# A fused encoder step on Trainium2: the opening rebuilt around x and c handed over transposed

## The reference

```python
def rmsnorm(x, gain):
    xf = x.astype(jnp.float32)
    y = xf * lax.rsqrt(jnp.mean(xf * xf, axis=-1, keepdims=True) + EPS)
    return (y * gain.astype(jnp.float32)).astype(x.dtype)

def mixer_layer(x, c, pos, past, w_ada, b_ada, ln_gain, w_in, ...):
    mod = jnp.einsum('bd,de->be', jax.nn.silu(c), w_ada) + b_ada
    shift, scale, gate = jnp.split(mod, 3, axis=-1)
    h = rmsnorm(x, ln_gain) * (1 + scale[:, None]) + shift[:, None]
    proj = jnp.einsum('btd,de->bte', h, w_in)
    ...
    q_a, ckv, krope, g_a, q_b, k_b, v_b, q_i, k_i, w_i, g_b = jnp.split(proj, split_at, axis=-1)
    # group A: latent attention from q_a, ckv, krope; group B: top-k sparse attention from q_b, k_b, v_b, q_i, k_i, w_i
    y = jnp.concatenate([rmsnorm(o_a, out_gain_a) * jax.nn.silu(g_a),
                         rmsnorm(o_b, out_gain_b) * jax.nn.silu(g_b)], axis=-1)
    out = jnp.einsum('bte,ed->btd', y, w_out)
    return x + gate[:, None] * out, new_rows
```

## Time and profile before

| | |
|---|---|
| median of 3 runs | 923.52 us |
| profiled execution | 923.6 us, span 921.8 us |
| TensorE (PE) busy | 884.2 us, 96% |
| weight loads (PEld) | 763.3 us, 83% |
| VectorE (DVE) busy | 416.6 us, 45% |
| ScalarE (ACT) busy | 321.6 us, 35% |
| GpSimd (POOL) busy | 124.2 us, 13% |
| chain that ended last | PE 84%, DVE 2%, ACT 2% of the span |
| loads of `ada` units | 64 x 512 KB, all in the first eighth |

### The profile page before, as it was taken

How to read it: one execution, slowest core, us unless ns; L and a number is a source line. 1 busy time by engine, 2 the same in 40 slices (tenths; PEclk the granted TensorE clock), 3 DMA queues, 4 the chain that set the end, 5 groups by cost and what they waited for, 6 DMA issues and landing times.

```text
span 921.8 us, 13576 instructions
## 1 busy us (share of the span) xinstructions
PE 884.2 (96%) x5485; PEld 763.3 (83%) x5485; DVE 416.6 (45%) x847; ACT 321.6 (35%) x598; POOL 124.2 (13%) x192
## 2 busy tenths in 40 slices
PE   4799999999999999999999999999999999999996
PEld 1376788999998688888999888888988898778885
DVE  3522343336322145433331576238645466697362
ACT  3222343434322234322321344233233345544251
POOL 1000003101200000112220300003012124450000
PEclk9899999999999999999999999999999999999998
DMA  8999957474443222556543666547878743793413
GB/s 342 409 409 409 408 190 231 157 243 159 143 137 103 69 92 69 186 174 213 186 137 107 206 235 230 207 149 226 292 250 256 253 143 109 274 295 116 137 57 126
DMA packets 53599, 187.43 MB, mean 203 GB/s; under 512 B 7872, under 2 KB 8568, under 8 KB 52384
## 3 DMA queue, kind: packets, MB, share of 16 engines
q1 hardware_dynamic: 39632, 141.85, 43.6%
q0 software_dynamic: 13904, 44.71, 15.4%
HBM read 175.93 MB, written 12.69 MB: 205 GB/s over the span
## 4 chain that ended last, share of the span: by engine, by line
PE 84%; DVE 2%; ACT 2%; issue 1%; POOLq 0%; DVEq 0%; POOL 0%; ACTq 0%
PE proj L1755 33%; PE proj L1744 29%; PE proj L1771 2%; PE bankO L1850 1%; PE bankO L1859 1%; PE proj L1728 1%; PE bankS L1771 1%; PE bankS L1744 1%; DVE w_lo L1272 1%; PE bankS L1913 1%; PE bankO L1940 1%; PE bankO L1932 1%; PE bankO L1931 1%; PE bankO L1900 1%; PE bankS L1956 1%
## 5 line engine op out<-in xcount | busy, mean ns | idle before, releaser
L1272 DVE TENSOR_TENSOR w_lo<-raw,w_hi 128x1024 fp32r<-128x1024 f32 (+2 forms) x164 | 198.7, 1217 | 236.2 <-ACT w_hi L954 235.4
L954 ACT ACTIVATE w_hi<-raw 128x1024 fp32r<-128x1024 f32 (+2 forms) x164 | 167.4, 1027 | 188.8 <-PE proj L1744 109.6
L1755 PE MATMUL proj<-hT_hi,w_hi 128*128 128x384 f32 x608 | 210.8, 347 | 0.0
L1755 PE MATMUL proj<-hT_hi,w_lo 128*128 128x384 f32 x608 | 203.7, 335 | 0.0
L1755 PE MATMUL proj<-hT_lo,w_hi 128*128 128x384 f32 x608 | 203.4, 335 | 0.0
L1744 PE MATMUL proj<-w_hi,hT_hi 128*128 128x512 f32 (+2 forms) x464 | 178.5, 385 | 2.8 <-DVE w_lo L1272 1.5
L1744 PE MATMUL proj<-w_hi,hT_lo 128*128 128x512 f32 (+2 forms) x464 | 173.8, 375 | 0.0
L1744 PE MATMUL proj<-w_lo,hT_hi 128*128 128x512 f32 (+2 forms) x464 | 173.8, 374 | 0.0
L1755 PEld LDWEIGHTS proj<-hT_hi,w_hi 128*128 128x128 f32 x608 | 114.2, 188 | 9.4 <-issue 7.8
L1755 PEld LDWEIGHTS proj<-hT_lo,w_hi 128*128 128x128 f32 x608 | 114.3, 188 | 0.6 <-issue 0.2
L1755 PEld LDWEIGHTS proj<-hT_hi,w_lo 128*128 128x128 f32 x608 | 114.1, 188 | 0.0
(11 more groups left out here) (357 smaller groups left out, 1022.4 us busy)
## 6 DMA issues: line engine op xcount, KB each, us to landing
raw<-in_units SPq DMA_DIRECT2D x184, 512.0 KB, 3.7
araw<-in_units SPq DMA_DIRECT2D x64, 512.0 KB, 9.5
kcT<-in_dsa_k_t POOLq DMA_DIRECT2D x8, 512.0 KB, 5.8
vc<-in_cache_dsa_v POOLq DMA_DIRECT2D x8, 512.0 KB, 5.6
gate_scratch<-stage POOLq DMA_DIRECT2D x8, 384.0 KB, 3.3
raw<-in_units SPq DMA_DIRECT2D x8, 336.0 KB, 4.0
raw<-in_units SPq DMA_DIRECT2D x8, 320.0 KB, 5.0
x_sb<-in_x_prompt SPq DMA_DIRECT2D x2, 1024.0 KB, 6.6
```

Source lines behind the costliest of these rows:

```text
L954: return nc.scalar.activation(out, in_, func, scale=scale, **kw)
L1272: V.tensor_tensor(w_lo[:, SLOT[u], 0:w], raw_of(u)[:, 0:w], high(u)[:, 0:w].bitcast(F32), ALU.subtract).then_inc(lo_ready, 1)
L1755: ins = mm(banks[blk][:, 0:TOK], w[:, n, cols], a[:, kt, :], start=first and n == m == 0, stop=final and n == per - 1 and m == 2)
```

## The change

x and c are laid out transposed before the launch (`x_t`, `c_t`), and so are the gains and biases (`gains_t`). x is loaded straight into `xsT` in four parts of four blocks. The squares are taken there, two parts on ScalarE and two on VectorE, and summed over the partitions by 16 products with a matrix of ones into 32-row groups (`xss`); a second product with ones adds the groups (`rb`), ScalarE takes the root, VectorE the reciprocal, over 384 columns on all partitions. Eight multiplications (`xm`) then scale `xsT`, one per pair of blocks. The transposes of x and c are gone.

The first `ada` chunk becomes two, `ade` 0 and 1: eight units each, with two blocks by 256 shift and 256 scale columns in a unit, so products have 128 columns and there are eight per unit. Each gives one pair of blocks. The chunks `ga` 0 and 1 become one chunk `gp` of 512 columns: a unit covers two blocks and four banks, so it needs one pair. Product units now stand inside `ade` 1 and `ada` 1 to 3.

```diff
-    out = [("ada", q, 1, 1) for q in range(4)]
-    out += [("kb", 0, 2, NT), ("ga", 0, 4, 2), ("ga", 1, 4, 2), ("ckv", 0, 2, NT), ...]
+    out = [("ade", e, 2, 1) for e in range(2)] + [("ada", q, 1, 1) for q in range(1, 4)]
+    out += [("kb", 0, 2, NT), ("gp", 0, 2, 4), ("ckv", 0, 2, NT), ...]
...
-    out = of("ada", 0)
-    for q in range(1, 4):
-        ada = of("ada", q)
-        out += ada[:4] + [keys[2 * q - 2]] + ada[4:8] + [first[q - 1]] + ada[8:12] + [keys[2 * q - 1]] + ada[12:]
-        out.append(second[q - 1])
-    out += [keys[6], keys[7], first[3], second[3]]
+    half = of("ade", 1)
+    out = of("ade", 0) + half[:3] + [keys[0]] + half[3:6] + [gates[0]] + half[6:]
+    ada = of("ada", 1)
+    out += ada[:5] + [keys[1]] + ada[5:10] + [gates[1]] + ada[10:]
+    for q in range(2, 4):
+        ada, n = of("ada", q), 2 * q - 2
+        out += ada[:4] + [keys[n]] + ada[4:8] + [gates[n]] + ada[8:12] + [keys[n + 1]] + ada[12:] + [gates[n + 1]]
+    out += [keys[6], keys[7], gates[6], gates[7]]
...
-        order.insert(max(first, at - AHEAD), u)
+        order.insert(max(first, at - (3 if u < second else 5 if u < third else 6)), u)
...
-    put(0, ("xsq", 0), ("xsq", 1), ("xsq", 2), ("xr", 0))
+    put(0, ("xsq", 0), ("xsq", 1), ("xsq", 2), ("xsq", 3), ("xss", 0))
     put(1, ("rb", 0))
-    run(1, "xT", 6, 2)
-    run(2, "xS", 6, 2)
+    put(2, ("xm", 0), ("xm", 1))
+    for m in range(2, 8):
+        put(m + 1, ("xm", m))
...
+    for n, mod in enumerate(MODS):
+        u = LAST_UNIT[mod]
+        pairs = [m for m in range(KT // 2) if MOD_OF_PAIR[m] == n]
+        put(u, ("modT", n))
+        if n == 0:
+            put(u, ("first_hi", 0))
+        put(u, *(("h", m) for m in pairs))
+        if n == 0:
+            put(u, ("first_lo", 0))
+        put(u, *(("hl", m) for m in pairs))
...
+        for n in range(4):
+            blocks = slice(4 * n, 4 * n + 4)
+            sp.dma_start(xsT[:, blocks, :], i["x_t"][:, blocks, :]).then_inc(sem(f"x_in{n}"), 16)
...   # VectorE
+        def xsq(n):
+            if n % 2:
+                part = xsT[:, 4 * n:4 * n + 4, :]
+                dve.wait_ge(sem(f"x_in{n}"), 16)
+                V.tensor_tensor(xsqr[:, 4 * n:4 * n + 4, :], part, part, ALU.mult).then_inc(sem(f"x_sq{n}"), 1)
+        def rb(n):
+            emptied(dve, "rb", n)
+            link(V.reciprocal(rbc[:], rbc[:]))
+        def xm(m):
+            part = xsT[:, 2 * m:2 * m + 2, :]
+            V.tensor_tensor(part, part, rbc[:].unsqueeze(1).broadcast_to([P, 2, TOK]),
+                            ALU.mult).then_inc(sem("x_scaled"), 1)
...   # TensorE
+            if (kind, j) in MODS[1:] and first:
+                emptied(pe, "modT", MODS.index((kind, j)) - 1)
+        def xss(n):
+            out = take("xss", n, "S")
+            for q in range(4):
+                pe.wait_ge(sem(f"x_sq{q}"), 1)
+                for g in range(4):
+                    ins = mm(out[32 * g:32 * (g + 1), 0:TOK], ones[:, 0:32], xsqr[:, 4 * q + g, :], start=q == 0,
+                             stop=q == 3)
+            ins.then_inc(full["S"], 1)
```

More of the change, by code:

```diff
@@ L117, in rings @@
     for u, (c, _) in enumerate(UNITS):
-        ada = CHUNKS[c][0] == "ada"
+        ada = CHUNKS[c][0] in ("ade", "ada")
         slot = RAW + counts[1] % ARAW if ada else counts[0] % RAW
@@ L127 @@
 SLOT, SLOT_BEFORE = rings()
-AHEAD = 6
 def loads():
     order = list(range(len(UNITS)))
-    first, last = (UNITS.index((CHUNK_OF["ada", q], k)) for q, k in ((1, 0), (3, KT - 1)))
-    for u in [u for u in order if CHUNKS[UNITS[u][0]][0] != "ada" and u < last + 3]:
+    first = UNITS.index((CHUNK_OF["ade", 1], 0))
+    second = UNITS.index((CHUNK_OF["ada", 1], 0))
+    third = UNITS.index((CHUNK_OF["ada", 2], 0))
+    last = UNITS.index((CHUNK_OF["ada", 3], KT - 1))
+    for u in [u for u in order if CHUNKS[UNITS[u][0]][0] not in ("ade", "ada") and u < last + 3]:
         at = order.index(u)
         order.remove(u)
-        order.insert(max(first, at - AHEAD), u)
+        order.insert(max(first, at - (3 if u < second else 5 if u < third else 6)), u)
     return order
 LOADS = loads()
-WHOLE = ("ada", "gate")
+WHOLE = ("ade", "ada", "gate")
 SPLIT_UNITS = [u for u, (c, _) in enumerate(UNITS) if CHUNKS[c][0] not in WHOLE]
@@ L163, in banks @@
     for kind, j, _, nb in CHUNKS:
-        if kind == "ada":
+        if kind in ("ade", "ada"):
             mine = [NPB]
@@ L399, in packed_units @@
         dst = out[u, :, 0:per * n].reshape(P, per, n)
-        if kind == "ada":
+        if kind == "ade":
+            for a in range(2):
+                dst[:, :, 256 * a:256 * (a + 1)] = w_ada[:, ks, a * D + 256 * j:a * D + 256 * (j + 1)]
+        elif kind == "ada":
             for a in range(2):
@@ L1315, in modT_ @@
[L1315 to L1316 removed]
+            k0, k1 = MOD_BLOCKS[n]
+            w = 32 * (k1 - k0)
+            part = modT[:, :, k0:k1, :]
+            dve.wait_ge(sem("small_in"), 48)
+            b_cols = gcol[:, 32:64].rearrange("p (a k) -> p a k", a=2)[:, :, k0:k1]
             for a in range(2):
[L1318 to L1319 removed]
+                ins = V.tensor_tensor(part[:, a], bank["O"][:, w * a:w * (a + 1)].rearrange("p (k j) -> p k j", j=32)[:, :, 0:9],
+                                      b_cols[:, a].unsqueeze(2).broadcast_to([P, k1 - k0, 9]), ALU.add)
@@ L1722, in products @@
                 clear(0)
-                for g in range(4):
+                for n, g in itertools.product(range(2), range(4)) if kind == "ade" else ():
+                    cols = raw_of(u).rearrange("p (a n) -> p a n", a=2)[:, n, P * g:P * (g + 1)]
+                    ins = mm(banks[0][32 * g:32 * (g + 1), 0:P], cs[:, 2 * k + n, :], cols, start=first and n == 0,
+                             stop=final and n == 1)
+                for g in range(4) if kind != "ade" else ():
                     if kind == "ada":
@@ L1748, in products @@
             else:
-                for blk in range(2):
+                for blk in range(nb):
                     cols = slice(P * blk, P * (blk + 1))
```

210 lines of the change are left out of this document (78 added, 132 removed), and 2 rows, old and new, of the table STEP_BANKS.

## The result

The changed kernel takes 928.58 us in the median of six runs (928.15 to 931.77); the kernel before takes 923.75 beside it. The ratio is 1.0057, with a 95% interval of 1.0047 to 1.0068. Five more runs gave 929.07 (ratio 1.0066, 1.0052 to 1.0079). It is slower by 4.8 to 5.5 us, about 0.6%. The direction is as forecast and the time lies in the range of 923.6 to 929.8, but the forecast itself was 926.8, that is 3.3 us: the loss is half as large again or more.

What follows compares the result with a forecast made beforehand. TensorE bounds the kernel from 116 us, so its delay in the opening moves the total. Chain 2.4 plus clock 0.9 = 3.3 us on the profiled 923.6 gives 926.9, median 926.8; range 923.6 to 929.8.

Steps and rivals of the forecast that it cites:

- The new wait: Opening: TensorE's transposes, ready at about 24.5 us, wait 6 us for VectorE's reciprocal and xm multiplications.
- First and second kb unit: Opening: the first kb unit starts at 34.1 us, 9.5 us earlier than before, the second at 51.8.
- The third kb unit: Starts at 73.4 us against 70.98, 2.4 us later, as the product unit covering its chain was taken earlier.
- The clock: TensorE's clock falls once more ahead of the third kb unit, charged 0.9 us.
- main case: Whole kernel: later by the chain and the clock, 926.8 us, own range 925.4 to 928.6, chance 0.56.
- The clock falls in every gap: Rival, opening: second and third kb unit pay 2 us each and loads run short, 929.9 us; chance 0.12.
- my own rule: TensorE's gaps: the clock falls only after gaps as empty as the one seen in the rows.
- The loads: Opening: a late ada ring may leave DMA engines short for a microsecond near 40 us; landings have slack.
- theories A of e3 and A' of e4: Experiment forecasts, opening gaps: restoring cover gives 924.5 to 926 us; keeping the clock up by fill gives 924 to 926.
- Faster: Rival, opening: VectorE ready sooner, TensorE held by the data alone, 922.6 us, at the limit 920.9; chance 0.08.
- What is worth nothing: Opening: dropped x transposes, ade units, the single gp store and a late ada ring change nothing in the total.
- The signs of being wrong: modT before 27 us, third kb unit before 71 us, or the end moving by another amount than that unit.

Runs made afterwards that it cites:

- Long profile: First profiled execution of the changed kernel, TensorE's clock low behind three gaps: 931.77 us.
- typical: Second profiled execution of the changed kernel, near the median, TensorE's clock low behind two gaps: 928.66 us.
- e5: Changed kernel with a ring of 14 instead of 8 buffers for ada loads: 930.25 us.
- e3: Changed kernel with the two gp units back behind the transposes as cover: 927.67 us.
- e4: Changed kernel with useless products behind the first, second and third transposes to keep TensorE busy: 928.44 us.
- e2: Changed kernel with only the first of eight xm multiplications ahead of the first modT on VectorE: 924.80 us.
- e6: Changed kernel with the edits of e3 and e5 together: 922.77 us.
- e7: Changed kernel with the edits of e2 and e3 together, ring of 8: 923.62 us.
- e8: e7 with scale, shift, high and low part of a quarter's second pair behind the split of the next kb unit's weights: 923.43 us.
- e10: e6 with the shorter chain edit of e8: 922.73 us.
- e1: Changed kernel with the halves undone, four ada quarters and the earlier unit order and load lead again; x path and gp stay: 923.97 us.

## Why the prediction came out right, and where it did not

*The new wait.* Right. Predicted: transposes ready at 24.5, a wait of 6 us, modT at 30.5. Long profile 25.02, 6.15, 31.19; typical 24.27, 5.76, 30.05. The ones-products, put at 4.1 us, took 3.7 to 5.3 in the runs, within the bounds given. (The upper bound, 6.5, was too wide: it took the 1.08 us of one set with its tail for the distance between sets; three `ade` units back to back on the low clock take 2.79 us, 0.86 apart.)

*First and second kb unit.* Predicted 34.1 and 51.8; typical 33.77 and 52.49, long 34.92 and 54.26.

*The third kb unit.* The main term, 2.4 us later by the cover that is gone: typical 74.02, 3.0 later. The chain behind the transposes is as forecast, 7.22 us against 7.25; the 0.6 us more came ahead of them, from the first `kb` unit (6.28 us against 5.23). But the view of the wait was incomplete. I expected 4 us for `w_lo`. TensorE waited 3.2 us for three late `ada` loads instead and was through with them at 73.87, while VectorE finished `w_lo` of this unit, the first of the two here, at about 73.96:

```profile
72.74 2.36 DVE L1279 TENSOR_TENSOR w_lo<-raw,w_hi 128x1024 fp32r<-128x1024 f32 x2
```

Two limits ended within 0.1 us of each other. With the loads on time (e5) the wait is the forecast one, 4.45 us for `w_lo`. That the loads, which I had as early, ended no later than the chain was luck.

*The clock.* The term that was mis-sized. I charged 0.9 us at the third unit, 2.0 at most; it cost 1.9 us there in the long and 2.3 in the typical profile (6.28 and 6.64 us instead of 4.34). The first unit took 6.28 to 6.90, where I had the 5.23 of before. The sum of 3.0 and 2.3 is the 5.35 us of the last transposes, against 3.3 predicted. My range for the main case, 925.4 to 928.6, just holds one of the medians (928.58) and misses the other (929.07). The error was to take the price from a unit of which only 2 us lay in a low stretch (43.65 to 45.7). In the long profile the products of the first unit stay slow from 34.9 to 40.5 us, 5.6 us of it, and those of the third from 77.3 to about 81.5.

*The clock falls in every gap* (0.12) came out half true, and its 929.9 lies nearer to both medians than my 926.8. The Trainium skill ("TensorE: Matmul & The Clock Gate", "HAM oscillation — how this bites in real kernels") has each group of a loop that waits for its loads start on the half clock; the runs stand between that and my own rule. The gap before the third unit was followed by the low clock in both profiles. The one before the second was in the long profile (5.86 us) and not in the typical one (4.35).

*The loads.* "May leave the DMA engines short for a microsecond near 40 us" was wrong in size, and "the data do not hold this up: they are there at 61.8" was wrong for the changed kernel. The engines stood at 0.17 for 4 us in the long profile and at 0.50 in the typical one. It was no part of the loss on its own (e5), so the forecast survived it. But it made my theories A of e3 and A' of e4 wrong, by which the cover or the clock alone is worth its term. The working that was missing is how long eight buffers last, 8 by 1.28 us, when TensorE reads nothing for 6 us and then little for 7.

*Faster* (0.08) had the right floor and the wrong condition. I wrote that it decides with modT before 25.5 us. e2 has modT at 24.98 and still 924.80; e6 has it at about 30 and 922.77. The floor of 922.6 set by the second quarter's landing at 61.8 is what e6, e7, e8 and e10 reach, to about 1 us.

*What is worth nothing.* Confirmed by e1 for the x path and the gate units, which it keeps at 923.97. The `ade` units, which e1 does not have, take 1.44 us for three on the full clock (41.82 to 43.26), 0.48 each against the 0.465 of an `ada` unit.

*The signs of being wrong.* One of them came up. I wrote that I am wrong if the end moves by another amount than the third `kb` unit does. Its start moved by 3.0 us and the span by 5.1 in the typical profile, 6.3 and 8.1 in the long one. The sum itself already put 0.9 us of clock inside that unit, so the sign was badly drawn; but the difference, 1.8 to 2.1 us, is the mis-sized term. The other signs held: modT at 30 to 31 us, and a granted clock of 0.50 from 30 to 34 us and 0.52 from 72 to 76 in the typical profile.

One thing stays open: why the low clock follows one gap and not a like one.

## What to carry to other kernels

When two chains are about equally long, taking away either one shows little or nothing, and it is easy to call a real cost harmless. Before believing a null result, look in its profile for what the engine waits for now, and try the pair. Look too at what the experiment itself delays, as the fill of e4 did with the loads. And where a change makes the consumer stand still, count how long the ring of buffers keeps the loads going, not only whether the data in it are early: a wait at 25 us left the DMA engines short of work at 40.
